# Gated retention rows of block two turned three items behind their tile instead of two, with a third buffer

## The reference, cut to what matters

```
scores = einsum(q, k) * decay_in            # within a chunk of 128 rows
inner  = einsum(scores, v)
state  = chunk_decay * state + einsum(k * zeta, v)
cross  = einsum(q, state_before, xi)
o = inner + cross
o = o * rsqrt(mean(o * o) + EPS)            # per head
o = o * silu(gate)
mixed = concat([o, attention]) @ w_out
```

## Time and profile before

| | us |
|---|---|
| median of 3 runs | 3180.6 (3179.82 to 3183.84) |
| the profiled execution's own time | 3181.32 |
| its span, first to last instruction | 3179.2 |
| PE busy | 2939.3 (92% of the span) |
| DVE, ACT, POOL busy | 1315.5, 1045.8, 1012.6 |

### The profile page before, as it was taken

The page is one execution under the profiler, slowest core; times in us unless marked ns, Lnnn a source line. Parts: engine busy times, 40 slices in busy tenths (PEclk is TensorE's granted clock), DMA queues, the critical chain, the costliest instruction groups (busy, mean ns, idle before and its releaser), DMA issues. The chain is left out here.

```text
span 3179.2 us, 37512 instructions
## 1 busy us (share of the span) xinstructions
PE 2939.3 (92%) x14048; PEld 2431.6 (76%) x14048; DVE 1315.5 (41%) x2088; ACT 1045.8 (33%) x1863; POOL 1012.6 (32%) x700
## 2 busy tenths in 40 slices
PE   2999999999999999999997987879999999998998
PEld 2878887887788888787885766758777888886877
DVE  6646557222700000114658876543445322323143
ACT  3215545002510000024545564334443222222243
POOL 2011122334523333245521132420063333332454
PEclk9999999999999999999999998857999999998999
DMA  5531112323311111133411130000061111112342
GB/s 182 192 100 34 28 40 61 92 67 119 133 40 46 46 52 47 39 120 126 140 47 40 47 106 27 21 0 1 1 205 47 53 46 53 46 46 73 96 146 90
DMA packets 196107, 230.17 MB, mean 72 GB/s; under 512 B 11657, under 2 KB 140809, under 8 KB 195977
## 3 DMA queue, kind: packets, MB, share of 16 engines
q1 hardware_dynamic: 195976, 228.44, 22.5%
HBM read 203.24 MB, written 25.17 MB: 72 GB/s over the span
## 5 line engine op out<-in xcount | busy, mean ns | idle before, releaser
L133 PE MATMUL psum<-sb_h_hi,sb_w_hi 128*128 128x512 f32 x1792 | 709.4, 396 | 13.9 <-POOL sb_w_lo L928 8.7
L135 PE MATMUL psum<-sb_h_hi,sb_w_lo 128*128 128x512 f32 x1792 | 702.3, 392 | 0.0
L134 PE MATMUL psum<-sb_h_lo,sb_w_hi 128*128 128x512 f32 x1792 | 701.7, 392 | 0.0
L1539 POOL TENSOR_TENSOR sb_out_lo<-sb_out_raw,sb_out_hi 128x512 fp32r<-128x512 f32 (+1 forms) x180 | 323.5, 1804 | 396.0 <-ACT sb_out_hi L1529 395.9
L133 PEld LDWEIGHTS psum<-sb_h_hi,sb_w_hi 128*128 128x128 f32 x1792 | 339.1, 189 | 86.5 <-POOL sb_w_lo L928 9.9
L133 PE MATMUL psum<-sb_out_hi,sb_a_hi 128*128 128x512 f32 x960 | 383.3, 399 | 19.5 <-DVE sb_a_lo L1534 10.6
L135 PEld LDWEIGHTS psum<-sb_h_hi,sb_w_lo 128*128 128x128 f32 x1792 | 338.8, 189 | 71.9
L134 PEld LDWEIGHTS psum<-sb_h_lo,sb_w_hi 128*128 128x128 f32 x1792 | 339.2, 189 | 68.4
L926 POOL TENSOR_SCALAR sb_w_hi<-sb_w_raw 128x1024 fp32r<-128x1024 f32 x97 | 102.4, 1055 | 895.3 <-PE psum L135 615.2
L134 PE MATMUL psum<-sb_out_lo,sb_a_hi 128*128 128x512 f32 x960 | 379.0, 395 | 0.0
L135 PE MATMUL psum<-sb_out_hi,sb_a_lo 128*128 128x512 f32 x960 | 378.8, 395 | 0.0
(11 more groups left out here) (392 smaller groups left out, 4389.9 us busy)
## 6 DMA issues: line engine op xcount, KB each, us to landing
sb_w_raw<-in_w_up SPq DMA_DIRECT2D x44, 512.0 KB, 3.8
sb_late_w<-in_w_ada SPq DMA_DIRECT2D x32, 512.0 KB, 4.8
sb_w_raw<-in_w_in SPq DMA_DIRECT2D x56, 256.0 KB, 3.0
sb_w_raw<-in_w_ffn_gate SPq DMA_DIRECT2D x22, 512.0 KB, 3.8
sb_w_raw<-in_w_ffn_up SPq DMA_DIRECT2D x22, 512.0 KB, 3.8
sb_out_raw<-in_w_ffn_down SPq DMA_DIRECT2D x22, 512.0 KB, 3.5
sb_out_raw<-in_w_ffn_down SPq DMA_DIRECT2D x44, 256.0 KB, 3.0
sb_out_raw<-in_w_down SPq DMA_DIRECT2D x22, 512.0 KB, 3.5
```

The costliest lines, as they stand in the source:

```text
L133: nc.tensor.matmul(out, stationary.hi, moving.hi, start=start, stop=False)
L134: nc.tensor.matmul(out, stationary.hi, moving.lo, start=False, stop=False)
L135: return nc.tensor.matmul(out, stationary.lo, moving.hi, start=False, stop=stop)
L1539: self.nc.gpsimd.tensor_tensor(w.lo, raw, w.hi.bitcast(F32), ALU.subtract).then_inc(self.w_lo, 1)
```

## The change

The gated rows of tile t are turned in item G_(t+3) instead of G_(t+2). So G2 turns none, G3 to G7 turn tiles 0 to 4, and A0, A1 and A2 turn tiles 5, 6 and 7. The list of turns, PE's and ACT's programs and the wait ahead of the SiLU follow. The gate rows get three buffers. The third lies where `gt` of the top-k lies, so DVE waits in A1, ahead of `above_at(0)`, until tile 5's gated rows, the last to use it, are turned.

```diff
@@ turn_outputs, and gated and scaled alike
-            last = self.nc.tensor.transpose(self.core.ps[:, 3, j * P:(j + 1) * P], self.gr[:, r % 2, j * P:(j + 1) * P], self.cst["ident"])
+            last = self.nc.tensor.transpose(self.core.ps[:, 3, j * P:(j + 1) * P], self.gr[r % 3][:, j * P:(j + 1) * P], self.cst["ident"])
...
@@ spread_phase
         for t in range(TB):
-            turns += [(K_, t)] + ([(G_, t - 2)] if t >= 2 else [])
-        turns += [(G_, TB - 2), (G_, TB - 1)]
+            turns += [(K_, t)] + ([(G_, t - 3)] if t >= 3 else [])
+        turns += [(G_, TB - 3), (G_, TB - 2), (G_, TB - 1)]
...
@@ PE
                         steps(n, 0, 3)
-                        if t >= 2:
-                            turn_free((G_, t - 2))
-                            ret.turn_outputs(pe, t - 2).then_inc(turned, 1)
+                        if t >= 3:
+                            turn_free((G_, t - 3))
+                            ret.turn_outputs(pe, t - 3).then_inc(turned, 1)
                         if t >= 1:
                             ret.outputs(pe, t - 1)
...
                     elif c == A_:
-                        if t < 2:
-                            turn_free((G_, TB - 2 + t))
-                            ret.turn_outputs(pe, TB - 2 + t).then_inc(turned, 1)
+                        if t < 3:
+                            turn_free((G_, TB - 3 + t))
+                            ret.turn_outputs(pe, TB - 3 + t).then_inc(turned, 1)
                         if t == 0:
                             ret.outputs(pe, TB - 1)
...
@@ DVE
                     if j in range(NP_):
                         top.choose(dve, chain, j)
+                    if j == -1:
+                        dve.wait_ge(turned, place[G_, TB - 3] + 1)
                     if j + 1 in range(NP_):
                         top.above_at(dve, chain, j + 1)
...
@@ ACT
-                        if t >= 2:
-                            turn_done((G_, t - 2))
-                            ret.outputs_out(t - 2).then_inc(turn_out, 1)
+                        if t >= 3:
+                            turn_done((G_, t - 3))
+                            ret.outputs_out(t - 3).then_inc(turn_out, 1)
...
-                    elif c == A_ and t < 2:
-                        turn_done((G_, TB - 2 + t))
-                        ret.outputs_out(TB - 2 + t).then_inc(turn_out, 1)
+                    elif c == A_ and t < 3:
+                        turn_done((G_, TB - 3 + t))
+                        ret.outputs_out(TB - 3 + t).then_inc(turn_out, 1)
...
-                        if t >= 2:
-                            act.wait_ge(turned, place[G_, t - 2] + 1)
-                        nc.scalar.activation(ret.gr[:, t % 2, :], core.ps[:, n % 3, :], ACT.Silu).then_inc(act_read, 1)
+                        if t >= 3:
+                            act.wait_ge(turned, place[G_, t - 3] + 1)
+                        nc.scalar.activation(ret.gr[t % 3][:, :], core.ps[:, n % 3, :], ACT.Silu).then_inc(act_read, 1)
...
@@ block_kernel
-        kr, vr, gr = (lay(FREE + 26.5 + 4 * n, name, [P, 2, RH * HD]) for n, name in enumerate(("k_rows", "v_rows2", "gate_rows")))
+        kr, vr = (lay(FREE + 26.5 + 4 * n, name, [P, 2, RH * HD]) for n, name in enumerate(("k_rows", "v_rows2")))
+        gr = [lay(FREE + kb, f"gate_rows{n}", [P, RH * HD]) for n, kb in enumerate((34.5, 36.5, 79.375))]
```

More of the change, by code:

```diff
@@ L2482, in gated @@
         dve.wait_ge(act_read, silu_at)
-        gr = self.gr[:, r % 2, :]
+        gr = self.gr[r % 3][:, :]
         nc.vector.tensor_tensor(gr, gr, self.core.ps[:, 6, :], ALU.mult).then_inc(self.o_read, 1)
@@ L2491, in scaled @@
     def scaled(self, dve, r):
-        gr = self.heads(self.gr[:, r % 2, :])
+        gr = self.heads(self.gr[r % 3][:, :])
         dve.wait_ge(self.root, 2 * r + 2)
```

## The result

The changed kernel takes 3163.75 us in the median of 5 runs (3159.37 to 3168.06), the kernel before 3180.6 on the same chip: ratio 0.9944, 95% interval 0.9931 to 0.9956. Measured a second time, 12 runs against 31, it is 3167.85 against 3182.46, ratio 0.996 (0.994 to 0.998). Over both, the means are 3166.9 (17 runs) and 3180.5 (36 runs), 13.6 us apart, by resampling 10 to 17. Single runs scatter: 3158 to 3180 of the changed kernel, 3156 to 3190 of the one before (84 runs with those taken beside the later experiments, median 3181.2). The forecast was 3174.0 with 3167 to 3179.5: too small a gain.

The account below looks back on a forecast made before the run. PE's 25.4 us of waits for DVE's scaling in G2, G4, G6 and A0 were taken as the bound. From 3181.3, less 7.8 gained, plus 1.2 for the clock, less 0.7 to the median: 3174.0, range 3167 to 3179.5.

Parts of the forecast that it names:

- Where the stalls are and what takes their place: PE's scaling waits (25.4 us) give way to decay in G2 and A0, the keys' copy in G4 and G6.
- The sum without the clock: G2 2.7, G4 1.46, G6 1.46 and A0 2.8 gained, less 0.56 for A2's added turning: 7.8 us gained.
- the clock's term of 1.2: Low clock behind the four stalls: 1.2 us lost, weighing a longer G2 stretch against the clock staying up in G4 or G6.
- The sum's lower bound: Gain if L2415 doesn't move ahead of the stall in G2 and A0: 3.7, also written 3.6 us.
- The clock in the stage: PE's low-clock stretches from L2420 after G2, G4, G6, A0: sum 25.7 us before, 26 to 32 expected.
- G2's short stretch: Low clock behind G2's stall, 1.5 us; if like the others' mean of 8.1, it costs 3.3 us; chance 0.18.
- the last of the sum: Whole kernel: profiled execution 3181.3, less 7.8 gain, plus 1.2 clock, less 0.7 to reach the median: 3174.0 us.
- a shift at A2 that doesn't reach the end: Sign of a wrong forecast: L2622 in A2, expected about 7 us earlier, without that shift carrying to the end.
- The first rival: The clock doesn't fall in G4 or in G6: 3167.9 us, with both 3163.0; chance 0.17.

Follow-up runs that it names:

- delayb: The kernel before with one extra POOL product of 128x384 ahead of the sparse attention; 3173.4 us, ratio 0.9988.
- delayb1: The kernel before with one extra POOL product of 128x640 ahead of the sparse attention; 3167.5 us, ratio 0.9973.
- late2: The kernel before with PE's turning of the gated rows behind outputs and ACT's squares ahead of its copy; 3162.5 us, ratio 0.9945.
- early2: The kernel before with DVE's decay(t) and scaled(t-1) both moved behind the first search step; 3172.5 us, ratio 0.9983.
- earlylate2: The kernel before with decay and scaling behind the first search step and the turning behind outputs; 3159.0 us, ratio 0.9943.
- again: The changed kernel, unedited, measured a second time in 12 runs; 3167.9 us, ratio 0.9960.
- late3: The changed kernel with PE's turning of the gated rows behind outputs and ACT's squares ahead of its copy; 3160.7 us, ratio 0.9931.
- delay1: The changed kernel with one extra POOL product of 128x384 ahead of the sparse attention; 3163.3 us, ratio 0.9958.
- early3: The changed kernel with DVE's decay(t) moved behind the first search step of its item; 3156.1 us, ratio 0.9910.
- earlylate: The changed kernel with decay behind the first search step and the turning behind outputs; 3139.7 us, ratio 0.9886.
- delay3: The changed kernel with three extra POOL products of 128x512 ahead of the sparse attention; 3173.7 us, ratio 0.9983.
- delay6: The changed kernel with six extra POOL products of 128x512 ahead of the sparse attention; 3155.0 us, ratio 0.9932.

## Why the prediction was wrong

- **Where the stalls are and what takes their place**: right. Stalls of 5.08, 4.16, 4.15 and 6.00 stand where 5.1, 4.15, 4.15 and 5.8 were forecast, on the engines named, and no wait appeared in the odd items or ahead of L2415.
- **The sum without the clock**, 7.8: it held. With the clock's term of 1.2 it said 6.6 at A2, and A2's turn_parts came at 2030.67 in place of 2036.82, 6.15 earlier, with G0 0.2 earlier: 5.9 in the stage. (The sum's lower bound is given as 3.7 and as 3.6; its terms add to 3.5, and no time hangs on the difference.) The stage in three traces of the kernel before (its own, delayb, delayb1) is 155.1, 155.9 and 158.3; in five of the changed one 149.2, 149.3, 149.0, 146.8, 146.5: means 8.3 apart.
- **The clock in the stage**: right in kind. The stretches at 0.50 behind L2420, against the earlier trace rows, are:

```profile
1916.70:1924.60 7.90, 7.90 (x30) 6.92 (x30) 5.48 (x13) 2.32 (x6) 2.37 (x3) 0.50 0.18 54
1948.10:1955.30 7.20, 7.20 (x31) 6.79 (x30) 3.81 (x10) 1.66 (x4) 1.71 (x2) 0.50 0.11 22
1979.20:1986.00 6.80, 6.80 (x31) 6.47 (x29) 3.42 (x10) 1.31 (x3) 1.29 (x2) 0.50 0.08 9
2008.40:2016.80 8.40, 8.36 (x32) 7.68 (x33) 0.68 (x1) 3.48 (x7) 8.40 (x8) 0.50 0.46 125
```

Their sum went from 25.7 to 30.3 us, a cost of 2.3 where 1.2 was taken; G2's short stretch did become like the others. But it was an accident of the one trace from which it was read. In delayb and delayb1, whose code in this stage is that of the kernel before, the stretch behind G2's L2420 is:

```profile
1919.20:1926.40 7.20, 7.20 (x31) 6.81 (x30) 2.40 (x7) 1.74 (x4) 1.78 (x2) 0.50 0.07 22
1921.80:1929.80 8.00, 8.00 (x34) 6.96 (x32) 2.81 (x8) 2.45 (x6) 2.49 (x3) 0.50 0.20 61
```

With 7.2 or 8.0 in G2 the sum before would be 31.4 or 32.2. Against that the change costs nothing at the clock, which fits the 8.3 between the means of the stage. The rule of the Trainium skill (TensorE: Matmul & The Clock Gate, Part 4), that transposes don't count for the clock as other matmuls do, isn't contradicted: in the changed kernel G2 has no transposes behind its stall and G4 and G6 have them, and the stretches are 7.9, 7.2 and 6.8. No run isolates it.

- **The step that failed** is the last of the sum, 3181.3 - 7.8 + 1.2 - 0.7 = 3174.0, read with "a shift at A2 that doesn't reach the end" as the one thing that could go wrong behind A2. It took the rest of the kernel, 1142.4 us in the trace before, as fixed. It is not: it was 1124.5 to 1142.4 in the nine traces without an added wait, with the same work in it, and 1132.4 and 1135.2 in the changed kernel's two: 10 and 7 us that stand in no term of the sum. They don't come from the third buffer. late2 and early2, on two buffers, have a rest of 1124.5 and 1124.7, and delayb1, the kernel before with nothing but a wait, one of 1126.6. The trace of before had, with earlylate2's, the longest rest of all, so a move of its arrival was likely to be a gain; so far as the traces show, that part of the gain is luck and not the edit's. The clock term looked only at the stretches behind the four stalls, 26 us at the low clock, and not at the 89 us at 0.50 in the sparse attention, which was there to see in the page's clock line.
- **The first rival**, with its 3163.0 for both stalls, had nearly the measured time (3163.75) and was wrong in its mechanism: the clock fell in G4 and G6 as before. A number that fits doesn't show its cause.

What stays open: what lets the clock rise in the sparse attention after 38, 57, 62, 85, 89 or 103 us. Two added waits put it at 57 as expected. One thing orders the traces: how long the clock had been low when the first scores began. It was 13.7 to 13.9 us in the three where the low stretch went on for 85 (after, again, delayb), 14.2 to 14.7 in the five where it went on for 57 (late2, late3, early2, delay1, delayb1), and 13.1 in the two of 89 and 103 (before, earlylate2). The other four have 12.6 (early3, 62), 15.8 (earlylate, 56), 16.7 (delay3, 89) and 19.7 (delay6, 38). Both of the first two groups hold kernels with an added wait and without, on two buffers and on three, so the extra idle time of PE is not what matters there. But this was seen behind the runs and no run was chosen to test it. And each kernel but the changed one has one trace, so how the 13.6 us of mean gain divide, 6 to 8 in the stage and the remainder behind it or ahead of it, is known from traces and not from all the runs.

## What to carry to other kernels

When a wait is removed, look in program order at the next wait of the same engine on the same late producer: here decay stood 0.6 us ahead of the scaling, and 19.4 of 25.4 us of stall stayed. Take away all that stands on the late step at once, since single edits only rename it. And where a program has a long stretch at the low clock, its time depends on when it gets there: split the time by stage in both traces before giving a gain to an edit, and hold a gain of under half a percent for real only if the stage that was edited shows it.

## What the runs showed of the hardware

The granted clock stayed at 0.50 for 103 us with PE busy 93% of them (95.28 of 102.90 us in earlylate2), in the sparse attention with its narrow matmuls. A wait of 5.9 us added ahead of that stage made the whole 13 us shorter (delay6, 3155.0 beside 3167.9). And the same code behind the same stall, G2 of the kernel before, ran at 0.50 for 1.5, 7.2 and 8.0 us in three traces.
